# Seven products of combined operands in the second feed-forward projection of inner blocks, weight highs of those products on ScalarE

## Chip, cores, metric

One core of one Trainium2 chip. The metric is the device time of one execution in microseconds (us), as the median of several runs. All tensors are fp32. Engine names in profile rows: PE (TensorE matmul), PEld (TensorE weight load), DVE (VectorE), ACT (ScalarE), POOL (GpSimd), SPq (the queue from which SyncE issues DMAs). ps is PSUM.

## What is computed

A trunk of two layers (a Conformer convolution module, then an mLSTM) over 1024 prompt and 32 decode tokens. After its mixer each layer has the same squared-ReLU feed-forward network, with D_MODEL = 1024 and D_FF = 4096:

```
x = _layer_norm(DN_ALPHA * x + mix, p['ln_mix_g'][i], p['ln_mix_b'][i])
hid = jnp.square(jax.nn.relu(x @ p['ffn_w1'][i]))
x = _layer_norm(DN_ALPHA * x + hid @ p['ffn_w2'][i], p['ln_ffn_g'][i], p['ln_ffn_b'][i])
```

The change concerns only how `hid @ ffn_w2` is worked out.

## The kernel before

**Layout.** Activations stand transposed: the partition is the feature, the columns are the 1056 tokens, cut into three chunks of CW = 352 columns. X holds the residual stream in fp32.

**Precision.** An fp32 operand is used as two fp32r parts: a high part (a rounding copy) and a low part (the operand less its high part). A product of a 128x128 weight tile with 352 columns is three matmuls (`product`, L403 to L405): weight high by data high, weight high by data low, weight low by data high. AH, AL are the parts of the normalised input, HH, HL those of the hidden activations, WH, WL those of the weights.

**Weight panels.** SyncE loads a 512 KB panel into one of two raw buffers RAW (`load_panel`), GpSimd writes its high part into WH and then its low part into WL, each of 1024 columns (`split_panel`, L388 and L390), in one of four slots. Semaphores tie them: w_raw (panel landed), w_free (TensorE has released slots, counted by `free_panels`), w_split (low part written, which TensorE waits for).

**The feed-forward stage.** D_FF is cut into FB = 8 blocks of 512 hidden features. In each, the *hidden part* makes 12 outputs (3 chunks by 4 tiles) of 8 tile products, 12 x 24 = 288 matmuls; the *second part* makes 24 outputs (3 chunks by 8 tiles of 128 model features) of 4 tile products, 24 x 12 = 288 matmuls. Four panels serve the first and four the second. ScalarE takes the relu out of PSUM into SGF (L716) and squares it into HH (L718); VectorE squares SGF in fp32 into SQF (L733) and subtracts HH to get HL (L736). VectorE adds each output of the second part into X (L753). The eighth block (`last`) runs chunk by chunk with the layer normalisation woven in, and the first block (`first`) runs its hidden part chunk by chunk behind the normalisation before; blocks 1 to 6 are a loop.

**Order.** Every engine runs its own list in program order, written out by hand; there is no scheduler. On ScalarE a block is `ffn_act` (12 times relu, square), on GpSimd `ffn_splits` (8 panels, in the order of use), on VectorE `ffn_dve` (12 times square, low part; then 24 additions), on TensorE `ffn_pe`.

Of the kernel before, what the change touches and what calls it, by code (L numbers as in the profile page):

```python
# [53 lines left out]
def program(nc, a, o):  # L54
    with ExitStack() as ctx:
# [195 lines left out]
        WKR = at("WKR", [P, NJ, 4, 4], F32, O_S + 4096)  # L251
        QKP = at("QKP", [P, NJ, 4, 4], F32, O_S + 4096 + 1024)
# [14 lines left out]
        w_hi = sem("w_hi")  # L267
        w_split = sem("w_split")
# [63 lines left out]
        wd_hi, wd_lo, wd_mm, wd_acc = sem("wd_hi"), sem("wd_lo"), sem("wd_mm"), sem("wd_acc")  # L332
# [30 lines left out]

        class Ff:
# [3 lines left out]
            def __init__(self, n):  # L368
                self.nmm, self.nh, self.nacc = n * FB * 36, n * FB * 12, n * FB * 24
# [7 lines left out]
        def load_panel(sp, n, cnt, k, src, width):  # L377

            wait(sp, w_split, n - 1)
            sp.dma_start(RAW[:, k % 2].rearrange("p (k f) -> p k f", f=width), src).then_inc(w_raw[k % 2], 16)  # L380

        def split_panel(pool, n, cnt, k):
# [6 lines left out]
            wait(pool, w_hi, n + 1)  # L389
            pool.tensor_tensor(WL[:, k % 4], RAW[:, k % 2], WH[:, k % 4].bitcast(F32), ALU.subtract).then_inc(w_split, 1)  # L390
# [223 lines left out]
        NP_F = [24, 24 + 64 + 48]  # L614

        def pn(n0, k, b):
            return n0 + k + 8 * b, (n0 + k) // 2 + 1 + 4 * b

        def ffn_loads(sp, l, b):
            w1, w2 = a["ffn_w1"][l], a["ffn_w2"][l]  # L620
            for k in range(8):
                n, cnt = pn(NP_F[l], k, b)
# [4 lines left out]
                load_panel(sp, n, cnt, k, src.rearrange("(k p) f -> p k f", p=P), width)  # L627

        def ffn_splits(pool, l, b):
            for k in range(8):  # L630
                split_panel(pool, *pn(NP_F[l], k, b), k)

# [8 lines left out]

        def ffn_pe(pe, l, b, first, last, before=None):

            F = ff[l]
            L = (ln_m0, ln_m1)[l]
            for i, (c, u, h) in enumerate(hidden_order(first)):
                k = 2 * u + h
                if c == 0:
                    pe.wait_ge(w_split, pn(NP_F[l], k, b)[0] + 1)
                release = None  # L650
                if first:
# [22 lines left out]
            def hidden_ready(c):  # L674
                n = F.nh + 4 * c + 4 if first else F.nh + 12 * b + 6 + 2 * c + 2
                pe.wait_ge(F.relu, n)
                pe.wait_ge(F.hl, n)

            def unit(c, u, i, bank, between=None):

                k = 4 + u
                pe.wait_ge(w_split, pn(NP_F[l], k, b)[0] + 1)
                for h in range(2):
                    release = None
                    if h == 0 and (i == 0 or (c == 0 and not last) or (c == 2 and u and last)):
                        release = (F.mm, F.nmm + 36 * b + 12 + 2 * i, 2 if i == 0 else 1)
                    product(pe, bank(h), k % 4, 256, h, HH, HL, 4, ch[c], release).then_inc(F.mm, 1)
                    if h == 0 and between:
                        between(c, u)
            if last:  # L690
                def by_chunk(c, u, between):
                    i = 4 * c + u
                    if u == 0:
                        hidden_ready(c)
                    if i >= 2:
                        pe.wait_ge(F.acc, F.nacc + 24 * b + 2 * (i - 1))
                    unit(c, u, i, lambda h: bank_of(c, u, h), between)
                ln_pe(pe, (ln_f0, ln_f1)[l], by_chunk, 4, F.acc, F.nacc + 24 * b)
                free_panels(pe, F.mm, F.nmm + 36 * b + 36, 1)
            else:  # L700
                for u in range(4):
                    for c in range(3):
                        if u == 0:
                            hidden_ready(c)
                        else:
                            pe.wait_ge(F.acc, F.nacc + 24 * b + 6 * (u - 1) + 2 * c + 2)
                        unit(c, u, 3 * u + c, lambda h: 2 * c + h)

        def ffn_act(act, l, b, first=False):
            F = ff[l]  # L710
            L = (ln_m0, ln_m1)[l]
            for i, (c, u, h) in enumerate(hidden_order(first)):
                act.wait_ge(F.mm, F.nmm + 36 * b + i + 1)
                wait(act, F.sq, F.nh + 12 * b + i - 1)
                wait(act, F.hh, F.nh + 12 * b + i - 1)
                act.activation(SGF[:, i % 2], ps[:, hidden_bank(first, c, u, h), 0:CW], ACT.Relu).then_inc(F.relu, 1)  # L716
                act.wait_ge(F.relu, F.nh + 12 * b + i + 1)
                act.activation(HH[:, 2 * u + h, ch[c]], SGF[:, i % 2], ACT.Square).then_inc(F.hh, 1)  # L718
# [5 lines left out]
                if first and i >= 5 and i % 2:  # L724
                    ln_prescale(act, L, i // 2 - 2) if i < 11 else None

        def ffn_dve(dve, l, b, first=False, last=False):
            F = ff[l]
            L = (ln_m0, ln_m1)[l]
            for i, (c, u, h) in enumerate(hidden_order(first)):  # L730
                dve.wait_ge(F.relu, F.nh + 12 * b + i + 1)
                wait(dve, F.hl, F.nh + 12 * b + i - 1)
                dve.tensor_tensor(SQF[:, i % 2], SGF[:, i % 2], SGF[:, i % 2], ALU.mult).then_inc(F.sq, 1)  # L733
                dve.wait_ge(F.hh, F.nh + 12 * b + i + 1)
                dve.wait_ge(F.sq, F.nh + 12 * b + i + 1)
                dve.tensor_tensor(HL[:, 2 * u + h, ch[c]], SQF[:, i % 2], HH[:, 2 * u + h, ch[c]].bitcast(F32),  # L736
                                  ALU.subtract).then_inc(F.hl, 1)
# [1988 lines left out]
```

## Time and profile before

| | us |
|---|---|
| median of 3 runs | 3169.58 (3167.16 to 3170.78) |
| the profiled execution | 3167.34 |
| its span, first to last instruction | 3165.6 |
| TensorE busy in the span | 3055.3 (97%) |
| VectorE, ScalarE, GpSimd busy | 1586.9, 790.2, 830.0 |
| mean granted clock of TensorE | 0.99 |

The profile is one execution. A row of its list of groups gives line, engine, operation, output and inputs, shape and count, then total busy time and the mean of one in ns, then the idle time of the engine before them and what ended it. The matmuls' own durations overlap one another, so the pace of TensorE is read from their start times. A row of the timeline gives start, duration, engine, line and operation, and in square brackets how long the engine had been idle and what released it.

### The profile page before, as it was taken

How to read it: one execution, taken by the hardware profiler on the slowest of the kernel's cores; microseconds unless marked ns; L12 is line 12 of the kernel's file. 1: busy time of each engine (PE TensorE's matmuls, PEld its weight loads, DVE VectorE, ACT ScalarE, POOL GpSimd, SP SyncE). 2: the span in 40 equal slices, each digit the busy share in tenths (PEclk: the TensorE clock that was granted, in tenths of full speed). 3: DMA queues.
4: the chain of work that ended last, by engine and by line, in shares of the span. 5: the costliest groups of instructions: out<-in, count | busy, mean ns of one | idle time of the engine just before them, and what ended most of it. 6: DMA issues, size and time to landing. Idle time of an engine off the chain costs nothing.

```text
span 3165.6 us, 50120 instructions
## 1 busy us (share of the span) xinstructions
PE 3055.3 (97%) x20024; PEld 2841.0 (90%) x20024; DVE 1586.9 (50%) x2318; ACT 790.2 (25%) x1475; POOL 830.0 (26%) x523
## 2 busy tenths in 40 slices
PE   7998899999999999999989999998999999999997
PEld 7885789999999998999967878777999999999996
DVE  4877454333333354443358687878227333333335
ACT  4000442011111124111144444534106111111113
POOL 2232113333323232333201110113414232333330
PEclk9999999999999999999989999999999999999999
DMA  7555311111111113323255564747311111111111
GB/s 217 148 133 138 94 33 54 47 46 46 46 40 50 43 41 119 119 101 114 85 181 205 203 237 179 251 162 278 102 35 54 41 53 40 53 46 46 46 34 55
DMA packets 277968, 317.92 MB, mean 100 GB/s; under 512 B 25877, under 2 KB 217621, under 8 KB 276610
## 3 DMA queue, kind: packets, MB, share of 16 engines
q1 hardware_dynamic: 257577, 250.01, 25.6%
q10 hardware_dynamic: 12960, 40.04, 3.3%
q0 software_dynamic: 7296, 25.96, 2.4%
q8 instruction: 98, 1.61, 0.2%
q14 instruction: 37, 0.30, 0.0%
HBM read 224.63 MB, written 92.19 MB: 100 GB/s over the span
## 4 chain that ended last, share of the span: by engine, by line
PE 79%; DVE 10%; ACT 6%; issue 4%; DMA 1%; SPq 0%; POOL 0%; another core or an unknown queue 0%; DVEq 0%; ACTq 0%; POOLq 0%
PE ps L403 23%; PE ps L404 22%; PE ps L405 22%; PE ps L2068 2%; PE ps L1128 2%; PE ps L1171 1%; DVE CB L2489 1%; ACT X L486 1%; DVE CT L1565 1%; PE ps L1137 1%; PE ps L1138 1%; DVE RST L1729 1%; PE ps L1139 1%; PE ps L424 1%; DVE HT L1747 1%
## 5 line engine op out<-in xcount | busy, mean ns | idle before, releaser
L403 PE MATMUL ps<-AH,WH 128*128 128x352 f32 x3072 | 1000.4, 326 | 6.2 <-ACT SO L849 4.1
L404 PE MATMUL ps<-AL,WH 128*128 128x352 f32 x3072 | 986.2, 321 | 0.0
L405 PE MATMUL ps<-AH,WL 128*128 128x352 f32 x3072 | 985.7, 321 | 0.0
L388 POOL TENSOR_SCALAR WH<-RAW 128x1024 fp32r<-128x1024 f32 x200 | 236.0, 1180 | 1663.5 <-PEq L410 1467.7
L403 PEld LDWEIGHTS ps<-AH,WH 128*128 128x128 f32 x3072 | 577.6, 188 | 31.5 <-issue 22.6
L404 PEld LDWEIGHTS ps<-AL,WH 128*128 128x128 f32 x3072 | 578.7, 188 | 1.1 <-issue 0.2
L405 PEld LDWEIGHTS ps<-AH,WL 128*128 128x128 f32 x3072 | 577.5, 188 | 0.0
L390 POOL TENSOR_TENSOR WL<-RAW,WH 128x1024 fp32r<-128x1024 f32 x200 | 517.3, 2587 | 16.7
L403 PE MATMUL ps<-HH,WH 128*128 128x352 f32 x1536 | 498.4, 324 | 0.0
L404 PE MATMUL ps<-HL,WH 128*128 128x352 f32 x1536 | 492.2, 320 | 0.0
L405 PE MATMUL ps<-HH,WL 128*128 128x352 f32 x1536 | 491.9, 320 | 0.0
L753 DVE TENSOR_TENSOR X<-X,ps 128x352 f32<-128x352 f32 x384 | 198.0, 520 | 465.7 <-PE ps L405 465.7
L716 ACT ACTIVATE SGF<-ps 128x352 f32<-128x352 f32 x192 | 89.1, 464 | 1121.9 <-PE ps L405 1121.8
L733 DVE TENSOR_TENSOR SQF<-SGF 128x352 f32<-128x352 f32 x192 | 137.5, 716 | 388.9 <-ACT SGF L716 388.6
L403 PEld LDWEIGHTS ps<-HH,WH 128*128 128x128 f32 x1536 | 288.1, 188 | 5.4 <-issue 4.6
L404 PEld LDWEIGHTS ps<-HL,WH 128*128 128x128 f32 x1536 | 288.6, 188 | 0.8
L405 PEld LDWEIGHTS ps<-HH,WL 128*128 128x128 f32 x1536 | 287.9, 187 | 0.0
L736 DVE TENSOR_TENSOR HL<-SQF,HH 128x352 fp32r<-128x352 f32 x192 | 197.1, 1027 | 20.0
L2489 DVE SCALAR_TENSOR_TENSOR CB<-U,PR,CB 128x32 f32<-128x32 f32 (+3 forms) x180 | 157.3, 934 | 0.7
L1171 PE MATMUL ps<-QT,XCH 128*128 128x256 f32 (+1 forms) x640 | 137.0, 358 | 0.0
L1171 PEld LDWEIGHTS ps<-QT,XCH 128*128 128x128 f32 x640 | 112.9, 190 | 13.8
L905 DVE SCALAR_TENSOR_TENSOR XC<-XM,PRM,XC 128x1024 f32<-128x1024 f32 x96 | 106.6, 1167 | 0.0
(317 smaller groups left out, 3392.3 us busy)
## 6 DMA issues: line engine op xcount, KB each, us to landing
RAW<-in_ffn_w SPq DMA_DIRECT2D x128, 512.0 KB, 3.6
CT<-in_state_mlstm_C SPq DMA_DIRECT2D x32, 1024.0 KB, 5.5
out_C_s<-CT SPq DMA_DIRECT2D x32, 1024.0 KB, 5.4
RAW<-in_ml_w_in SPq DMA_DIRECT2D x32, 512.0 KB, 3.9
RAW<-in_conv_w_pw SPq DMA_DIRECT2D x24, 512.0 KB, 7.9
STK<-u_scratch SPq DMA_DIRECT2D x64, 184.0 KB, 3.8
xc_scratch<-XC ACTq DMA_DIRECT2D x16, 528.0 KB, 2.7
so_scratch<-SO ACTq DMA_DIRECT2D x16, 528.0 KB, 3.7
```

Of the source, the lines that this page charges most:

```text
L388: pool.tensor_scalar(WH[:, k % 4], RAW[:, k % 2], 1.0, 0.0, ALU.mult, ALU.add).then_inc(w_hi, 1)
L390: pool.tensor_tensor(WL[:, k % 4], RAW[:, k % 2], WH[:, k % 4].bitcast(F32), ALU.subtract).then_inc(w_split, 1)
L403: pe.matmul(ps[:, bank, 0:CW], wh[:, k, cols], hi[:, k, cs], start=(k == 0), stop=False)
L404: pe.matmul(ps[:, bank, 0:CW], wh[:, k, cols], lo[:, k, cs], start=False, stop=False)
L405: mm = pe.matmul(ps[:, bank, 0:CW], wl[:, k, cols], hi[:, k, cs], start=False, stop=(k == nk - 1))
L716: act.activation(SGF[:, i % 2], ps[:, hidden_bank(first, c, u, h), 0:CW], ACT.Relu).then_inc(F.relu, 1)
L733: dve.tensor_tensor(SQF[:, i % 2], SGF[:, i % 2], SGF[:, i % 2], ALU.mult).then_inc(F.sq, 1)
L736: dve.tensor_tensor(HL[:, 2 * u + h, ch[c]], SQF[:, i % 2], HH[:, 2 * u + h, ch[c]].bitcast(F32), ALU.subtract).then_inc(F.hl, 1)
L753: dve.tensor_tensor(x, x, ps[:, bank, 0:CW], ALU.add).then_inc(F.acc, 1)
L905: ins = dve.scalar_tensor_tensor(o_, x_, PRM[:, j, t:t + 1], o_, ALU.mult, ALU.add)
L1171: mm = pe.matmul(ps[:, 3 + q % 2, o_:256], xch(h)[:, dt, i * P:(i + 1) * P], QT[:, dt, tc * 256 + o_:tc * 256 + 256], start=(dt == 0), sto ...
L2489: ins = dve.scalar_tensor_tensor(y, x(t), w, y, ALU.mult, ALU.add)
```

## The change

In blocks 0 to 6 of both layers (14 blocks), the second part treats chunks 0 and 1 together. For each pair of output tiles (four pairs a block, numbered g) the 2x2 block product [two output tiles] by [two chunks] is made with seven products M1 to M7 of combined operands in place of eight, each over two 128-deep tiles (6 matmuls where the eight had 6 each). Chunk 2 keeps two ordinary products of 12 matmuls (P0, P1). A pair is 7 x 6 + 2 x 12 = 66 matmuls, before 72.

**Weights.** For each pair GpSimd no longer makes both parts. ScalarE makes the high part of the plain panel (`corner_highs`, called at the end of `ffn_act`), GpSimd its low part, then four small operations of 128x256 that form the combined corners in RAW itself; ScalarE makes the high part of these and GpSimd their low part, in a second slot. A block has 12 panels of four slots where it had 8.

**Activations.** VectorE writes the squares to HR (the place of HL), forms combined tiles (`combine`), and writes low parts with larger operations; ScalarE rounds the combined tiles (`combined_highs`).

**Sums.** M1 is added to X and then M6, M7 and M4 go on in the same PSUM bank, each being added to another tile of X after the next product has joined. A pair has 9 additions where it had 6.

The buffers WKR and QKP of the block weights moved to other addresses, and the counts of semaphores changed everywhere accordingly.

```diff
+        def ffn_splits(pool, l, b, last=False):
+            for k in range(8 if last else 4):
+                split_panel(pool, panel_no(l, b, k), panel_in(l, b, k) // 16, k, split_no(l, b, k))
+            for g in range(0 if last else 4):
...
+                a11, a12, a21, a22 = (corner(raw, j, i) for i in range(2) for j in range(2))
+                pool.wait_ge(a_hi, na + 1)
+                pool.tensor_tensor(WL[:, 2 * g % 4], raw, WH[:, 2 * g % 4].bitcast(F32), ALU.subtract).then_inc(w_split, 1)
+                pool.wait_ge(w_split, n + 1)
+                pool.tensor_tensor(a22, a21, a22, ALU.add).then_inc(w_hi, 1)
+                pool.wait_ge(w_hi, q + 1)
+                pool.tensor_tensor(a21, a11, a21, ALU.subtract).then_inc(w_hi, 1)
...
+                pool.tensor_tensor(a12, a12, a11, ALU.subtract).then_inc(w_hi, 1)
+                pool.wait_ge(w_hi, q + 4)
+                pool.wait_ge(a_hi, na + 2)
+                pool.tensor_tensor(WL[:, (2 * g + 1) % 4], raw, WH[:, (2 * g + 1) % 4].bitcast(F32), ALU.subtract).then_inc(w_split, 1)
+
+        def corner_highs(act, l, b):
+
+            for g in range(4):
+                k, n, q = 4 + g, panel_no(l, b, 4 + 2 * g), split_no(l, b, 4 + 4 * g)
+                act.wait_ge(w_raw[k % 2], panel_in(l, b, k))
+                act.wait_ge(w_free, n - 3)
+                act.copy(WH[:, 2 * g % 4], RAW[:, k % 2]).then_inc(a_hi, 1)
+                act.wait_ge(w_hi, q + 4)
+                act.wait_ge(w_free, n - 2)
+                act.copy(WH[:, (2 * g + 1) % 4], RAW[:, k % 2]).then_inc(a_hi, 1)
...
+            def m1(g):
+                slot = weights(g, 0)
+                if g == 0:
+                    pe.wait_ge(F.relu, relu0 + (11 if first else 10))
+                    operand("corner")
...
+                added(g - 2, "M4")
+                seven(xbank(g), slot, 0, 0, *tile(0, 0), True, (F.mm, mm0 + 12, 2) if g == 0 else None)
+
+            def m4(g):
+                added(g, "M7")
+                operand("t")
+                seven(xbank(g), 2 * g % 4, 1, 1, *combined(1), False)
+
+            def m2(g):
+                added(g - 1, "M2")
+                seven(YB, 2 * g % 4, 1, 0, *tile(1, 0), True, (F.mm, mm0 + 12 + turn(g - 1, "M4") + 1, 2) if g else None)
+
+            def m5(g):
+                slot = weights(g, 1)
+                operand("t1")
+                added(g - 1, "M3")
+                seven(ZB, slot, 1, 1, *tile(0, 1), True)
...
+            for g in range(4):
+                m1(g)
+                if g:
+                    m4(g - 1)
+                m2(g)
+                m5(g)
+                plain(g, 0)
+                m6(g)
+                m3(g)
+                plain(g, 1)
+                m7(g)
+            m4(3)
...
+            if not last:
+                corner_highs(act, l, b)
...
+                dve.tensor_tensor(t3, b22, b12, ALU.subtract).then_inc(F.sq, 1)
+                dve.tensor_tensor(b12, b12, b11, ALU.subtract).then_inc(F.sq, 1)
...
+                dve.tensor_tensor(t2, b22, b12, ALU.subtract).then_inc(F.sq, 1)
...
+                dve.tensor_tensor(t4, b21, t2, ALU.subtract).then_inc(F.sq, 1)
...
+                low(HL[:, both, ch[0]], HR[:, both, ch[0]], HH[:, both, ch[0]])
...
+                low(HL[:, 2 * u, ch[1]], HR[:, 2 * u, ch[1]], HH[:, 2 * u, ch[1]])
...
+                low(TL[:, :, u], TR[:, :, u], TH[:, :, u])
+                low(HL[:, 2 * u + 1, ch[1]], HR[:, 2 * u + 1, ch[1]], HH[:, 2 * u + 1, ch[1]])
```

**What stands where.** ScalarE, the end of a block in the loop of layer 0, before: the last two relus (L716) and squares (L718), behind which the loop turns to the next block.

```order
234 L717 REGISTER_ALU
235 L718 ACTIVATE HH<-SGF 128x352 [waits ffn_relu]
236 L713 REGISTER_ALU
237 L716 ACTIVATE SGF<-ps 128x352 [waits ffn_hh,ffn_sq,ffn_mm]
238 L717 REGISTER_ALU
239 L718 ACTIVATE HH<-SGF 128x352 [waits ffn_relu]
240 L2350 REGISTER_ALU
241 L2350 COMPARE_AND_BRANCH
```

ScalarE at the same place, now. L906 and L909 are the relu and the square; L684 to L689 are `corner_highs`, of which the first of four pairs is shown, the next following at once.

```order
266 L901 REGISTER_ALU [waits ffn_mm]
267 L902 REGISTER_ALU [waits ffn_sq]
268 L906 ACTIVATE SGF<-ps 128x352 [waits ffn_hh]
269 L908 REGISTER_ALU
270 L909 ACTIVATE HH<-SGF 128x352 [waits ffn_relu]
271 L684 ISA
272 L685 REGISTER_ALU [waits w_raw0]
273 L686 CAST WH<-RAW 128x1024 [waits w_free]
274 L687 REGISTER_ALU
275 L688 REGISTER_ALU [waits w_hi]
276 L689 CAST WH<-RAW 128x1024 [waits w_free]
```

All eight roundings of the block's second-part weights stand behind the relu and square of its last hidden output.

GpSimd, the second half of the loop's body, before: the last three of four panels of the second part, each a high part (L388) that needs only a raw panel and a free slot, and a low part.

```order
80 L388 TENSOR_SCALAR WH<-RAW 128x1024 [waits w_free,w_raw1]
81 L51 REGISTER_ALU
82 L390 TENSOR_TENSOR WL<-RAW,WH 128x1024 [waits w_hi]
83 L51 ISA [waits w_free]
84 L388 TENSOR_SCALAR WH<-RAW 128x1024 [waits w_raw0]
85 L51 REGISTER_ALU
86 L390 TENSOR_TENSOR WL<-RAW,WH 128x1024 [waits w_hi]
87 L388 TENSOR_SCALAR WH<-RAW 128x1024 [waits w_free,w_raw1]
88 L51 REGISTER_ALU
89 L390 TENSOR_TENSOR WL<-RAW,WH 128x1024 [waits w_hi]
90 L1955 REGISTER_ALU
91 L1955 COMPARE_AND_BRANCH
```

GpSimd, the first pair's panel, now (L667 low part of the plain panel, L669 to L675 the combined corners, L678 their low part).

```order
109 L667 TENSOR_TENSOR WL<-RAW,WH 128x1024 [waits a_hi]
110 L668 REGISTER_ALU
111 L669 TENSOR_TENSOR RAW<-RAW 128x2x128 [waits w_split]
112 L670 REGISTER_ALU
113 L671 TENSOR_TENSOR RAW<-RAW 128x2x128 [waits w_hi]
114 L672 REGISTER_ALU
115 L673 TENSOR_TENSOR RAW<-RAW 128x2x128 [waits w_hi]
116 L674 REGISTER_ALU
117 L675 TENSOR_TENSOR RAW<-RAW 128x2x128 [waits w_hi]
118 L676 REGISTER_ALU
119 L677 REGISTER_ALU [waits w_hi]
120 L678 TENSOR_TENSOR WL<-RAW,WH 128x1024 [waits a_hi]
```

Each low part now waits for a_hi, the count of ScalarE's roundings, and the corners stand between the two low parts.

## Rows read from the trace of the kernel before

**Rows 1.** The page: span, busy time by engine, granted clock in 40 slices.

```profile
span 3165.6 us, 50120 instructions
...
PE 3055.3 (97%) x20024; PEld 2841.0 (90%) x20024; DVE 1586.9 (50%) x2318; ACT 790.2 (25%) x1475; POOL 830.0 (26%) x523
...
PEclk9999999999999999999989999999999999999999
```

**Rows 2.** Busy time in the halves of one block: window, length, then each engine.

```profile
541.66:587.42 45.76, 45.76 (x290) 45.76 (x290) 20.84 (x27) 11.57 (x24) 10.94 (x6) 1.00 0.12 35
587.42:633.22 45.80, 45.80 (x290) 45.80 (x290) 12.78 (x25) 0.00 (x1) 17.59 (x11) 1.00 0.20 58
```

**Rows 3.** Timeline, TensorE, from the hidden part into the second part.

```profile
583.12 0.32 PE L405 MATMUL ps<-AH,WL 128*128 128x352 f32 x1
583.28 0.32 PE L403 MATMUL ps<-HH,WH 128*128 128x352 f32 x1
```

**Rows 4.** Timeline, ScalarE: the block's last relu and square, the next block's first relu.

```profile
583.48 0.47 ACT L716 ACTIVATE SGF<-ps 128x352 f32<-128x352 f32 x1 [2.82 <-PE ps L405]
583.98 0.50 ACT L718 ACTIVATE HH<-SGF 128x352 fp32r<-128x352 f32 x1
633.22 0.47 ACT L716 ACTIVATE SGF<-ps 128x352 f32<-128x352 f32 x1 [48.74 <-PE ps L405]
```

**Rows 5.** Timeline, GpSimd: one panel of the second part.

```profile
595.29 1.05 POOL L388 TENSOR_SCALAR WH<-RAW 128x1024 fp32r<-128x1024 f32 x1 [4.01 <-PEq L410]
596.42 2.40 POOL L390 TENSOR_TENSOR WL<-RAW,WH 128x1024 fp32r<-128x1024 f32 x1
```

**Rows 6.** Groups by line and shape, whole run: durations for new operations.

```profile
L2269 ACT CAST AH<-X 128x1024 fp32r<-128x1024 f32 x8 | 8.4, 1048 | 0.3
...
L390 POOL TENSOR_TENSOR WL<-RAW,WH 128x1024 fp32r<-128x1024 f32 x200 | 517.3, 2587 | 16.7
...
L1945 POOL TENSOR_TENSOR SEL<-SEL,ident 128x32 f32<-128x32 f32 x2 | 0.5, 252 | 0.2
...
L494 DVE TENSOR_TENSOR AL<-X,AH 128x1408 fp32r<-128x1408 f32 x18 | 30.2, 1680 | 28.7 <-ACT AH L490 28.7
L1593 DVE TENSOR_TENSOR PL<-PT,PH 128x256 fp32r<-128x256 f32 x64 | 28.4, 444 | 1.9 <-ACT PH L1376 1.9
```

**Rows 7.** Timeline, TensorE: the first matmuls behind three longer waits.

```profile
1220.58 0.63 PE L403 MATMUL ps<-AH,WH 128*128 128x352 f32 x1 [4.08 <-ACT SO L849]
...
2184.79 0.49 PE L403 MATMUL ps<-AL,WH 128*128 128x352 f32 x1 [3.46 <-POOL WL L390]
...
2214.92 0.40 PE L403 MATMUL ps<-AL,WH 128*128 128x352 f32 x1 [4.00 <-POOL WL L390]
```

**Rows 8.** Timeline, GpSimd: the low parts that ended two of those waits.

```profile
2180.85 3.69 POOL L390 TENSOR_TENSOR WL<-RAW,WH 128x1024 fp32r<-128x1024 f32 x1
...
2212.43 2.34 POOL L390 TENSOR_TENSOR WL<-RAW,WH 128x1024 fp32r<-128x1024 f32 x1
```

**Rows 9.** Timeline, VectorE, one block: a low part alone, one beside GpSimd, an addition.

```profile
546.46 0.53 DVE L736 TENSOR_TENSOR HL<-SQF,HH 128x352 fp32r<-128x352 f32 x1
...
585.34 2.54 DVE L736 TENSOR_TENSOR HL<-SQF,HH 128x352 fp32r<-128x352 f32 x1
...
589.21 0.52 DVE L753 TENSOR_TENSOR X<-X,ps 128x352 f32<-128x352 f32 x1 [0.47 <-PE ps L405]
```

**Rows 10.** Windows behind those three waits; the third value from the right is the clock.

```profile
2188.00:2190.00 2.00, 2.00 (x12) 1.95 (x12) 1.55 (x6) 1.00 (x2) 0.49 (x1) 0.91 1.05 448
...
2214.00:2216.00 2.00, 1.08 (x6) 1.11 (x7) 0.00 (x0) 0.00 (x0) 1.92 (x3) 0.92 1.06 397
...
2218.00:2220.00 2.00, 2.00 (x11) 2.00 (x10) 0.00 (x0) 0.00 (x0) 0.24 (x1) 0.73 1.07 401
...
1224.00:1226.00 2.00, 2.00 (x9) 2.00 (x8) 0.00 (x0) 2.00 (x2) 0.00 (x0) 0.55 0.00 0
```

**Rows 11.** The page's DMA issues: panels of the feed-forward weights.

```profile
RAW<-in_ffn_w SPq DMA_DIRECT2D x128, 512.0 KB, 3.6
```

More of the change, by code:

```diff
@@ L626, in ffn_loads @@
                     src, width = w2[bass.ds(b * 512, 512), (k - 4) * 256:(k - 3) * 256], 256
[L627 to L631, printed above, removed]
+                if last or k < 6:
+                    done = n + k - 1 if k or (isinstance(b, int) and b == 0) else n - 2
+                else:
+                    done = n + 2 * k - 6
@@ L672, in ffn_pe, with hidden_ready @@
                     ln_var_sum(pe, L, 2)
[L674 to L689, printed above, removed]
             if last:
+                def hidden_ready(c):
+                    n = 6 + 2 * c + 2
+                    pe.wait_ge(F.relu, relu0 + n)
+                    pe.wait_ge(F.hl, hl0 + n)
                 def by_chunk(c, u, between):
                     i = 4 * c + u
+                    k = 4 + u
                     if u == 0:
@@ L695, in by_chunk @@
                     if i >= 2:
[L696 to L707, printed above, removed]
@@ L709, in ffn_act @@
-        def ffn_act(act, l, b, first=False):
+                        pe.wait_ge(F.acc, acc0 + 2 * (i - 1))
+                    pe.wait_ge(w_split, panel_no(l, b, k) + 1)
+                    for h in range(2):
+                        release = None
+                        if h == 0 and (i == 0 or (c == 2 and u)):
+                            release = (F.mm, mm0 + 12 + 2 * i, 2 if i == 0 else 1)
+                        product(pe, bank_of(c, u, h), k % 4, 256, h, HH, HL, 4, ch[c], release).then_inc(F.mm, 1)
+                        if h == 0:
+                            between(c, u)
@@ new lines, in ffn_pe, with seven @@
+                ln_pe(pe, (ln_f0, ln_f1)[l], by_chunk, 4, F.acc, acc0)
+                free_panels(pe, F.mm, mm0 + 36, 1)
+                return
+            def seven(bank, slot, j, i, hi, lo, start, release=None):
+                for k in range(2):
+                    if k == 1 and release:
+                        free_panels(pe, *release)
+                    wh, wl = corner(WH[:, slot], j, i)[:, k], corner(WL[:, slot], j, i)[:, k]
+                    pe.matmul(ps[:, bank, 0:CW], wh, hi(k), start=(start and k == 0), stop=False, skip_group_check=True)
+                    pe.matmul(ps[:, bank, 0:CW], wh, lo(k), start=False, stop=False, skip_group_check=True)
+                    mm = pe.matmul(ps[:, bank, 0:CW], wl, hi(k), start=False, stop=(k == 1), skip_group_check=True)
+                mm.then_inc(F.mm, 1)
@@ new lines, in ffn_dve @@
+            for i, (c, u, h) in enumerate(hidden_order(first)):
+                dve.wait_ge(F.relu, relu0 + i + 1)
+                if last:
+                    wait(dve, F.hl, hl0 + i - 1)
+                    dve.tensor_tensor(SQF[:, i % 2], SGF[:, i % 2], SGF[:, i % 2], ALU.mult).then_inc(F.sq, 1)
+                    dve.wait_ge(F.hh, hh0 + i + 1)
+                    dve.wait_ge(F.sq, sq0 + i + 1)
+                    dve.tensor_tensor(HL[:, 2 * u + h, ch[c]], SQF[:, i % 2], HH[:, 2 * u + h, ch[c]].bitcast(F32),
+                                      ALU.subtract).then_inc(F.hl, 1)
+                else:
+                    dve.tensor_tensor(raw(2 * u + h, c), SGF[:, i % 2], SGF[:, i % 2], ALU.mult).then_inc(F.sq, 1)
+                    if (c, h) == (1, 1):
+                        if l and first and u == 0:
+                            dve.wait_ge(d_out, 16 * (8 + HEADS))
+                        combine(u, i)
+                    if (c, h) == (2, 1):
+                        both = slice(2 * u, 2 * u + 2)
+                        dve.wait_ge(F.sq, sq0 + raw_order(first, i) + 1)
+                        dve.wait_ge(F.hh, hh0 + squared(first, i))
+                        low(HL[:, both, ch[2]], HR[:, both, ch[2]], HH[:, both, ch[2]])
@@ L2349, in _ @@
             ffn_act(act, 0, 0, True)
-            with act.Fori(1, FB) as b:
+            with act.Fori(1, FB - 1) as b:
                 ffn_act(act, 0, b)
+            ffn_act(act, 0, FB - 1, last=True)
             ln_act(act, ln_f0, R_FFNG, R_FFNB, 4)
```

272 lines of the change are left out of this document (204 added, 68 removed).

## Prediction, made before the changed kernel had run

> **What bounds the kernel now.** I read the page first: TensorE is busy 97% of the span and its clock is full nearly throughout; no other engine is busy more than half of it [rows 1]. Next, the windows of one block in the loop of layer 0: it takes 633.22 − 541.66 = 91.56 us, and TensorE is busy for all of both halves [rows 2, 4]. A block has 576 matmuls, so one costs 91.56/576 = 0.159 us, which is also the distance of two start times [rows 3]. So inside these blocks only two things count: how many matmuls there are, and whether TensorE ever waits. In the timeline it does not: the second part's first matmul follows the hidden part's last without a gap [rows 3], because the low part of its panel had long been made. GpSimd makes each panel one or two ahead, as soon as TensorE frees a slot, in 1.05 + 0.08 + 2.40 = 3.53 us [rows 5].
>
> **What the change removes.** Each pair loses 6 matmuls, a block 24, the kernel 14 x 24 = 336: 14 x 3.82 = 53.4 us. That is all it can win.
>
> **What it adds on TensorE's path: the first pair of each block.** I count time from the moment at which the second part would start, 583.28 in the trace before. The roundings of the weights now stand on ScalarE behind the block's last relu and square. That relu cannot start before TensorE has ended the hidden part: it starts at 0.20, and the square ends at 583.98 + 0.50 − 583.28 = 1.20 [rows 4]. Raw panel and slots were ready long before, but ScalarE comes to them only now. Then, in series:
> - high part, 1024 columns on ScalarE, 1.05 [rows 6]: from 1.25 to 2.30.
> - low part on GpSimd, 2.40 [rows 5]: from 2.36 to 4.76.
> - GpSimd to TensorE 0.15: the first row of [rows 7] that waited on a quiet low part began 0.15 after it (2214.92 against 2212.43 + 2.34, [rows 8]). M1 starts at **4.91** instead of 0.
> - the four corner operations of 256 columns. No row shows them; between 0.252 for 32 columns and 2.40 for 1024 a straight line gives 0.252 + 224 x 2.148/992 = 0.74, and with the group's mean of 2.59 it gives 0.78 [rows 5, 6]. I take 0.78 and 0.08 between two: 4.84 to 8.20. Bounds: 0.65 (a quarter of 2.59) and 1.05 (what 1024 columns with one input cost [rows 5]).
> - ScalarE high part, 8.27 to 9.32; GpSimd low part, 9.38 to 11.78. M5, which needs this second slot, starts at **11.93**.
> Without waits M5 would start 12 matmuls after M1, at 1.91. The pair is **10.02 us** late; 4.91 before M1 and 5.11 between M2 and M5.
>
> The Trainium skill, GPSIMD Engine Reference, section "Elementwise — side-by-side cycle accounting", gives 2.6 cycles at 1.2 GHz for each element of a two-input operation, from which I estimate 0.55 + 0.18 = 0.73 us a piece; the sum would be 14 x 4 x 0.05 = 3 us less. Its section "Engine selection" says that two-input elementwise work belongs to VectorE, about twice as fast. This speaks against the change: VectorE takes 0.44 for such a piece [rows 6], which would save 1.4 us of each of these waits, 19 us in all, had the change put them there.
>
> **The other pairs.** Slots of pair g+1 are freed behind the first matmuls of M2 of pair g, as GpSimd's release now comes 0.57 into a product (595.29 [rows 5], against 583.28 + 72 x 0.159 = 594.72). From there the same series runs: 0.57 + 0.05 + 1.05 + 0.07 + 2.40 + 4 x 0.86 + 0.07 + 1.05 + 0.07 + 2.40 + 0.15 = 11.32. M5 of pair g+1 comes 66 + 6 matmuls after that M2 starts, at 11.45. So it is just in time, by 0.13 us: no stall, but no cover either. Every 0.1 us more for a corner piece costs 0.3 to 0.4 in each of pairs 2 and 3. Pair 1 has slots free since M1 of pair 0 and is ready at 21.4 where M5 is due at 22.4.
>
> **The sums.** M4 of a pair must wait until M7's addition is done: 0.20 from the product's nominal end to the addition and 0.52 for it (589.21 is 0.20 behind the second product's end, 583.28 + 36 x 0.159 = 589.01 [rows 9]), 0.05 back: 0.77. In pairs 0 to 2 M1 of the next pair, 0.95, hides that; behind the last pair nothing does: **0.77 us** a block. The other additions have two products or more as cover. Their 36 x 0.52 = 19 us on VectorE lie beside 42 us of matmuls.
>
> **Activations.** VectorE has four more operations in each half of the hidden part, and ScalarE one rounding of 1056 columns. The last `combine` starts after output 10 of 12, at −7.6 (two products before the end). Relu, square, four operations of 0.53, then low parts of 704, 352, 1056 and 352 columns at 0.91, 0.53, 1.30, 0.53 (from 0.53 and 1.68 by a line [rows 6, 9]) end at about −0.6, and the rest, square 10, square 11 and the low part of chunk 2, at 2.3. All is before 4.91, and GpSimd starts at 2.36, so that VectorE is not held up beside it as in the row where a low part took 2.54 [rows 9]. This costs nothing, hidden by the wait for the weights; without that wait P0, the first to need chunk 2's low part, would start at 18 x 0.159 = 2.9, so it would cost nothing either. SyncE's loads come 3.6 us after issue [rows 11] and are asked for when a raw buffer's second low part is made, some 10 us ahead of use: nothing.
>
> **The clock.** Behind each of three waits of 3.46, 4.00 and 4.08 us the clock was 0.5 for a while, that is 1.2 of 2.4 GHz, and a matmul then cost 0.29. A window's mean tells how much of it was at half: 0.91 over 2 us is 0.36 us. So the low stretches that lay on busy time ran from 2184.79 to 2188.36, from 2215.7 to 2219.1 and from 1220.58 to 1225.8 [rows 7, 10]; half of each is lost: 1.8, 1.7, 2.6 us. The two new waits, 4.9 and 5.1 with only 12 matmuls between them, are longer than all of these. What M1 and M2 lose is hidden, since M5 waits for a fixed moment. Behind M5 I take **2.3 us**, to the upper end since two waits stand together; bounds 0 and 2.6. None of the three was spared, so I count all 14 blocks.
>
> The Trainium skill has a rule on it (TensorE: Matmul & The Clock Gate, section "HAM oscillation — how this bites in real kernels"): a loop that waits long in each turn pays for a fall of the clock in each turn. By it the sum would hold the clock's term 14 times too, and the rival without it has no place; the trace agrees in three of three waits.
>
> **The sum.** A block: −3.82 + 10.02 + 0.77 + 2.3 = +9.27 us; fourteen: +129.8. First blocks run their hidden part in another order, but their weights stand behind the last relu too, so I count them alike. The profiled execution was 3167.34, so 3297.1 for it; the median lies 2.2 above that execution: **3299 us**, 4% slower.
>
> **Rivals.**
> - *The clock stays up* (the waits are shorter than I think, or the fall passes while TensorE waits). For: in the second row of three the first matmuls were still at the full clock. Against: three of three in [rows 7, 10]. 14 x 2.3 = 32 less: 3267. Chance 0.13.
> - *The second slot's series is the bound in every pair.* With corner pieces at 1.05, each series is 1.08 longer: +1.1 in pair 0, and 11.32 + 1.08 − 11.45 = 0.95 in pairs 2 and 3: 3.0 a block, 42 in all: 3341. For: operations with short rows and two inputs that nobody timed, and a margin of 0.13. Against: the line through two rows. Half of it is as likely as the whole. Chance 0.13.
> - *The other side: weights in time.* If ScalarE made the first pair's roundings before its last relu, M1 and M5 would not wait, nor the clock fall: −3.82 + 0.77 a block, 3127. For: the panel lies in RAW and slots are free some 20 us ahead. Against: the order on ScalarE's list, which no wait can change. It turns to a gain where the waits in a block are under 3.8 us together; M1's alone is over that. Chance 0.03; no change, 0.01.
>
> **How the numbers follow.** Forecast 0.70. The range goes from a little under the rival without the clock's fall, 3258, to the dear corner pieces, 3340. A measurement of this kernel can tell about 0.2% from no change. Faster 0.03, same 0.01, slower 0.96.
>
> **What would show it.** Right: in each of 14 blocks TensorE idle twice, about 5 and (at a low clock less, 3.5) us, both put down to GpSimd's low part; 12 matmuls between; the clock below 1 behind; ScalarE's first rounding directly behind its last square; a loop's block of about 101 us. Wrong: a second-part start without idle time, idle time at M5 of later pairs, or the wait put down to VectorE's tiles or to a DMA.

## Result and the profile after

| | us |
|---|---|
| before, median of 4 runs | 3169.03 (3167.16 to 3170.78) |
| after, median of 4 runs | 3304.19 (3300.08 to 3309.79) |
| ratio | 1.0423, 95% interval 1.0411 to 1.0436 |
| span of the profiled execution, before and after | 3165.6, 3302.5 |

The change costs 135 us. It was to cost 130 (3299, range 3258 to 3340).

The page of the changed kernel, answering [rows 1]: 336 matmuls fewer (20024 less 19688), GpSimd and ScalarE busier, and TensorE busy for a smaller share of a longer span.

```profile
span 3302.5 us, 50982 instructions
...
PE 3068.2 (93%) x19688; PEld 2837.5 (86%) x19688; DVE 1643.8 (50%) x2570; ACT 930.9 (28%) x1615; POOL 1060.1 (32%) x747
```

TensorE's waits, longest groups first. Where [rows 3] had no gap there are now 14 of each kind: M1's (L667 is the plain low part), M5's (L678 the low part of the combined corners) and M4's (L1000 an addition). A line gives the time in total, how often, and the longest.

```profile
PE ps L786 <- POOL WL L667: 69.5, 14, 6.4
PE ps L786 <- POOL WL L678: 41.9, 14, 3.2
...
PE ps L786 <- DVE X L1000: 9.6, 14, 0.7
```

One block of the loop in layer 0, in the timelines. The last matmul of the hidden part:

```profile
797.78 0.32 PE L418 MATMUL ps<-AH,WL 128*128 128x352 f32 x1
```

The prediction's zero, 583.28, was the moment at which the second part would start, one distance of 0.16 behind the start of that matmul. Here it is 797.94, and every lateness below counts from there. Now ScalarE: the last relu and square, and behind them both roundings of pair 0 and the first of pair 1, in answer to [rows 4].

```profile
798.30 0.46 ACT L906 ACTIVATE SGF<-ps 128x352 f32<-128x352 f32 x1 [2.49 <-PE ps L418]
798.79 0.50 ACT L909 ACTIVATE HH<-SGF 128x352 fp32r<-128x352 f32 x1
799.20 1.03 ACT L686 CAST WH<-RAW 128x1024 fp32r<-128x1024 f32 x1
805.98 1.05 ACT L689 CAST WH<-RAW 128x1024 fp32r<-128x1024 f32 x1 [5.75 <-POOL RAW L675]
806.93 1.04 ACT L686 CAST WH<-RAW 128x1024 fp32r<-128x1024 f32 x1
```

GpSimd at the same place, answering [rows 5]. It had been idle for 40 us, and the last transfer of the panels that lay ready in RAW had ended at 764.

```profile
800.30 2.34 POOL L667 TENSOR_TENSOR WL<-RAW,WH 128x1024 fp32r<-128x1024 f32 x1 [40.48 <-ACT WH L686]
802.72 0.72 POOL L669 TENSOR_TENSOR RAW<-RAW 128x256 f32<-128x256 f32 x1
803.52 0.73 POOL L671 TENSOR_TENSOR RAW<-RAW 128x256 f32<-128x256 f32 x1
804.33 0.73 POOL L673 TENSOR_TENSOR RAW<-RAW 128x256 f32<-128x256 f32 x1
805.14 0.73 POOL L675 TENSOR_TENSOR RAW<-RAW 128x256 f32<-128x256 f32 x1
807.10 2.34 POOL L678 TENSOR_TENSOR WL<-RAW,WH 128x1024 fp32r<-128x1024 f32 x1 [1.23 <-ACT WH L689]
```

TensorE: the first matmul of M1, of M5, and of the last M4.

```profile
802.86 0.66 PE L786 MATMUL ps<-HH,WH 128*128 128x352 f32 x1 [4.75 <-POOL WL L667]
...
809.57 0.66 PE L786 MATMUL ps<-HH,WH 128*128 128x352 f32 x1 [3.20 <-POOL WL L678]
...
851.47 0.43 PE L786 MATMUL ps<-TH,WH 128*128 128x352 f32 x1 [0.70 <-DVE X L1000]
```

Read the three together: the hand-over goes TensorE, ScalarE's relu and square, ScalarE's rounding, GpSimd, TensorE, then GpSimd's corners, ScalarE, GpSimd, TensorE, and nothing in it overlaps the hidden part. M1 starts 4.92 late, and M5 11.63 behind the hidden part's end instead of 1.91. (The idle times in brackets are shorter, 4.75 and 3.20, since they count from the recorded end of a matmul and not from where the next would have started.) Over five blocks of the loop, first matmul of M1 at 601.50 to the same at 1106.47, a block takes 100.99 us where it took 91.56.

In the two first blocks M1 starts 6.3 and 6.5 late and M5 13.1 and 13.3. A scaling of X stands there on ScalarE's list ahead of the last two relus, and so ahead of the first rounding:

```profile
492.99 2.54 ACT L513 ACTIVATE X<-X 128x2816 f32<-128x2816 f32 x1
```

```profile
500.69 0.66 PE L786 MATMUL ps<-HH,WH 128*128 128x352 f32 x1 [6.10 <-POOL WL L667]
```

From the hidden part's end to the end of M4 these two blocks take 56.4 and 56.1 us where they took 45.8.

The clock around M5 (window, length, five engines, clock, DMA share, GB/s), answering [rows 10]:

```profile
809.00:811.00 2.00, 1.43 (x5) 1.44 (x6) 0.00 (x0) 0.00 (x0) 2.00 (x2) 0.55 0.11 36
811.00:813.00 2.00, 2.00 (x10) 2.00 (x9) 0.52 (x1) 0.00 (x0) 1.84 (x3) 0.60 0.67 226
813.00:815.00 2.00, 2.00 (x14) 2.00 (x13) 0.52 (x1) 0.00 (x0) 1.84 (x3) 1.00 0.00 0
```

M5 begins at 1.2 GHz and the clock is back at 2.4 some 3 us later.

### The profile page after: what moved, and what is told of

Same layout as the page of the kernel before. It is cut to its first block, busy times and chain, and to the rows that moved or that the text cites. A ratio compares the mean times of both kernels' runs of the same rounds, so it can differ in the third digit from the quotient of the medians.

```text
span 3302.5 us, 50982 instructions
## 1 busy us (share of the span) xinstructions
PE 3068.2 (93%) x19688; PEld 2837.5 (86%) x19688; DVE 1643.8 (50%) x2570; ACT 930.9 (28%) x1615; POOL 1060.1 (32%) x747
## 4 chain that ended last, share of the span: by engine, by line
PE 55%; issue 20%; DVE 11%; ACT 7%; POOL 5%; DMA 1%; PEld 0%; POOLq 0%; SPq 0%; another core or an unknown queue 0%; DVEq 0%; PEldq 0%; ACTq 0%
PE ps L416 11%; PE ps L417 11%; PE ps L418 11%; PE ps L786 4%; PE ps L787 4%; PE ps L788 4%; PE ps L2326 2%; PE ps L1421 1%; PE ps L1378 1%; ACT X L499 1%; DVE CB L2749 1%; POOL WL L403 1%; POOL WL L667 1%; POOL WL L678 1%; DVE CT L1815 1%
## 5 line engine op out<-in xcount | busy, mean ns | idle before, releaser
L1000 DVE TENSOR_TENSOR X<-X,ps 128x352 f32<-128x352 f32 x504 | 262.7, 521 | 483.8 <-PE ps L788 316.8
L401 POOL TENSOR_SCALAR WH<-RAW 128x1024 fp32r<-128x1024 f32 x144 | 174.0, 1208 | 835.3 <-PEq L423 637.5
L403 POOL TENSOR_TENSOR WL<-RAW,WH 128x1024 fp32r<-128x1024 f32 x144 | 377.6, 2623 | 12.0
L667 POOL TENSOR_TENSOR WL<-RAW,WH 128x1024 fp32r<-128x1024 f32 x56 | 133.4, 2381 | 650.6 <-ACT WH L686 650.6
L786 PE MATMUL ps<-HH,WH 128*128 128x352 f32 x448 | 162.7, 363 | 111.4 <-POOL WL L667 69.5
L966 DVE TENSOR_TENSOR HR<-SGF 128x352 f32<-128x352 f32 x168 | 89.7, 538 | 347.5 <-ACT SGF L906 347.3
L906 ACT ACTIVATE SGF<-ps 128x352 f32<-128x352 f32 x192 | 88.3, 462 | 610.3 <-PE ps L418 610.3
L416 PE MATMUL ps<-HH,WH 128*128 128x352 f32 x640 | 216.7, 339 | 0.0
L417 PE MATMUL ps<-HL,WH 128*128 128x352 f32 x640 | 212.0, 331 | 0.0
L418 PE MATMUL ps<-HH,WL 128*128 128x352 f32 x640 | 211.7, 331 | 0.0
L786 PEld LDWEIGHTS ps<-HH,WH 128*128 128x128 f32 x448 | 94.7, 211 | 120.7 <-issue 100.9
L788 PE MATMUL ps<-HH,WL 128*128 128x352 f32 x448 | 157.9, 352 | 0.0
L787 PE MATMUL ps<-HL,WH 128*128 128x352 f32 x448 | 157.8, 352 | 0.0
L678 POOL TENSOR_TENSOR WL<-RAW,WH 128x1024 fp32r<-128x1024 f32 x56 | 133.8, 2390 | 68.9 <-ACT WH L689 68.9
L689 ACT CAST WH<-RAW 128x1024 fp32r<-128x1024 f32 x56 | 58.7, 1049 | 344.6 <-POOL RAW L675 344.6
```

Of the source, the lines that this page charges most:

```text
L416: pe.matmul(ps[:, bank, 0:CW], wh[:, k, cols], hi[:, k, cs], start=(k == 0), stop=False)
L417: pe.matmul(ps[:, bank, 0:CW], wh[:, k, cols], lo[:, k, cs], start=False, stop=False)
L418: mm = pe.matmul(ps[:, bank, 0:CW], wl[:, k, cols], hi[:, k, cs], start=False, stop=(k == nk - 1))
L667: pool.tensor_tensor(WL[:, 2 * g % 4], raw, WH[:, 2 * g % 4].bitcast(F32), ALU.subtract).then_inc(w_split, 1)
L678: pool.tensor_tensor(WL[:, (2 * g + 1) % 4], raw, WH[:, (2 * g + 1) % 4].bitcast(F32), ALU.subtract).then_inc(w_split, 1)
L786: pe.matmul(ps[:, bank, 0:CW], wh, hi(k), start=(start and k == 0), stop=False, skip_group_check=True)
```

## Experiments

Each is the changed kernel with the edit shown, or one of these variants with one edit more, where the text says so. Times are medians, each compared with runs of the kernel before on the same chip. The variants ran on two chips, on which the kernel before took 3172.2 and 3169.2 us, so a difference in us between two variants can be off by some 3; the ratios allow for it.

### Who rounds: GpSimd instead of ScalarE

```diff
+                pool.wait_ge(w_raw[k % 2], panel_in(l, b, k))
+                pool.wait_ge(w_free, n - 3)
...
+                pool.tensor_scalar(WH[:, 2 * g % 4], raw, 1.0, 0.0, ALU.mult, ALU.add).then_inc(a_hi, 1)
                 pool.wait_ge(a_hi, na + 1)
...
                 pool.wait_ge(w_hi, q + 4)
+                pool.wait_ge(w_free, n - 2)
...
+                pool.tensor_scalar(WH[:, (2 * g + 1) % 4], raw, 1.0, 0.0, ALU.mult, ALU.add).then_inc(a_hi, 1)
                 pool.wait_ge(a_hi, na + 2)
...
-            if not last:
-                corner_highs(act, l, b)
```

> The changed kernel, but GpSimd makes the high parts of the second part's panels too, as it did before the change; ScalarE has none. Products, sums and activations are those of the change. Theory (the hand-over through ScalarE, whose list reaches it only behind the last relu, holds up M1 and M5 of pair 0): in the loop's blocks pair 0 is ready about 12 us ahead and both waits and the clock's fall go; a block costs -3.82 + 0.87 (M4's wait as the trace of after has it) = -2.95 us against before. In the two first blocks slots come free two products before the end only, so that M5 still waits some 1.6 us. 3169 - 41 + 3 = 3131. Rival (GpSimd's series itself, or its contention with VectorE's combining, is the bound): GpSimd has 1.05 us more twice a pair, so every later pair waits too: 3304 or more.

**Measured: 3190.34 us**, ratio 1.006 (1.0044 to 1.0077). Both waits are gone from the loop's blocks and 114 us with them, so the rival falls. But it stopped 59 us above the 3131 expected. The trace shows one new wait in each loop block, at P0. TensorE, then VectorE and GpSimd around it:

```profile
685.40 0.43 PE L416 MATMUL ps<-HH,WH 128*128 128x352 f32 x1 [1.88 <-DVE HL L939]
```

```profile
682.49 2.85 DVE L939 TENSOR_TENSOR HL<-HR,HH 128x704 fp32r<-128x704 f32 x1
```

```profile
682.08 2.52 POOL L672 TENSOR_TENSOR WL<-RAW,WH 128x1024 fp32r<-128x1024 f32 x1
684.68 1.26 POOL L674 TENSOR_TENSOR RAW<-RAW 128x256 f32<-128x256 f32 x1
```

The block's last low part on VectorE, for which P0 waits, takes 2.85 us instead of 0.89, lying beside GpSimd's low part of pair 1, which now starts as soon as M1 frees slots. It is what [rows 9] showed at 2.54 where nobody waited for it. The expectation had left it out. A loop block takes 91.0 us, or 92.6 where the clock falls behind the wait (8 of 12), against 88.6 expected: some 41 of the 59 us. The rest lies in the two first blocks, where P0 waits 4.8 us for the same low part and M1 2.35.

### Is that the sharing?

The variant above with one wait more: GpSimd begins the panel of pair 1 only behind VectorE's last low part.

```diff
                 pool.wait_ge(w_raw[k % 2], panel_in(l, b, k))
+                if g == 1:
+                    pool.wait_ge(ff[l].hl, ff[l].nhl + 10 * b + 10)
```

> gpsimd_highs with one wait more: GpSimd begins the panel of pair 1 only when VectorE has made its last low part of the block (chunk 2, second half). Theory (in gpsimd_highs that low part, 0.89 us alone, took 2.85 beside GpSimd's low part of pair 1, so that P0 waited 1.88 us, and the clock's fall behind it cost about 1.6 more): both go; pair 1 is begun some 1.5 us later, which its margin of about 1.3 us nearly takes. 12 loop blocks x 3.4 = 41 less, up to 0.3 of them back: 3190 - 41 + (0 to 4) = 3149 to 3153. Rival (VectorE is late by its own work, not by the sharing): 3190 or more.

**Measured: 3159.69 us**, ratio 0.9974 (0.9965 to 0.9983), 31 us less than without the hold (27 by the ratios). The low part is back at its own length, and the wait at P0 is gone:

```profile
679.23 0.89 DVE L941 TENSOR_TENSOR HL<-HR,HH 128x704 fp32r<-128x704 f32 x1
```

So it was the sharing, not VectorE's own work: a GpSimd instruction put later made the kernel faster. The gain is less than the 41 expected for two reasons that the trace shows. Another 0.75 to 0.80 us of idle time appears in each loop block some 13 us behind the hidden part's end (at 601.10, 691.12, 781.13), at M5 of pair 1: its panel is now begun later, and the panel's second low part ends 0.13 ahead of it. (The profile puts the wait down to an addition that ends 0.02 later, for which M5 does not wait.) And the clock had fallen behind that wait of 1.88 in 8 of 12 loop blocks only.

```profile
598.60 2.37 POOL L689 TENSOR_TENSOR WL<-RAW,WH 128x1024 fp32r<-128x1024 f32 x1
```

```profile
601.10 0.43 PE L797 MATMUL ps<-HH,WH 128*128 128x352 f32 x1 [0.75 <-DVE X L1009]
```

A loop block takes 90.0, 2.05 less on the mean, or 25 us in all. Some 8 more come from the two first blocks, which the expectation had not counted: P0's wait of 4.8 us there is 0.4 and 0.7 now.

### Where on ScalarE's list

ScalarE keeps the roundings; only the place of pair 0's two moves.

```diff
+                if not last and i == (10 if first else 6):
+                    corner_high(act, l, b, 0, 0)
+                if not last and i == (11 if first else 8):
+                    corner_high(act, l, b, 0, 1)
...
             if not last:
-                corner_highs(act, l, b)
+                for g in range(1, 4):
+                    corner_high(act, l, b, g, 0)
+                    corner_high(act, l, b, g, 1)
```

> The changed kernel with the two ScalarE roundings of pair 0 moved up on ScalarE's list: in the loop's blocks behind the squares of hidden outputs 7 and 9, in first blocks behind those of outputs 11 and 12 (there the slots come free no sooner). Nothing else. Theory (the place on the list alone is the fault): loop blocks as with GpSimd's highs, -2.95 us; first blocks keep a wait of about 6 us at M5 and 1.5 us of low clock, +15 us in all; 3169 - 41 + 15 = 3143. Rival (moving them delays the relus and the combined activations as much, since ScalarE waits for GpSimd's corners at the second): stays over 3200.

**Measured: 3158.69 us**, ratio 0.9959 (0.9945 to 0.9973): 145 us less than the changed kernel, by two instructions a block that stand elsewhere, and faster than the kernel before. In the loop's blocks TensorE's only wait is M4's. TensorE's waits in this kernel:

```profile
PE ps L787 <- POOL WL L667: 10.2, 2, 5.2
PE ps L787 <- DVE X L1007: 9.6, 14, 0.7
...
PE ps L787 <- POOL WL L678: 7.2, 2, 3.6
```

Of the 15 us above the 3143 expected some 12 lie in the two first blocks, where M1 and M5 still wait 5.2 and 3.6: I had thought M1 free there. The last pairs of outputs come close together, and ScalarE has a scaling of X (2.55 us) between them. The rest is 0.3 us in each loop block, 88.93 where 88.6 was expected.

### The two waits apart

Only the first rounding moved (`i == 6`, in first blocks 10), the second left behind the last square.

> Only the first rounding of pair 0 is moved up (behind the square of hidden output 7; in first blocks of output 11); the second stays behind the last square. It tells the two waits apart. Theory: M1 waits no more; M5 is ready at 1.25 + 1.05 + 0.05 + 2.40 + 0.15 = 4.9 where it is due at 1.91, a wait of 2.9 us. If a wait of 2.9 us costs no clock, a loop block is -3.82 + 0.87 + 2.9 = -0.05 and the whole about 3178 (first blocks +4.5 each); if it does, 1.5 us more in each of 12 blocks, 3196. Rival (the two waits are one delay, and what M1 gains M5 loses): 3290 to 3304.

**Measured: 3203.77 us**, ratio 1.0109 (1.0089 to 1.0129). M1 does not wait in the loop's blocks, M5 waits 2.8 to 3.1 us; so they are two delays, each with its own hand-over, and the rival falls. M5 of pair 0 in three blocks in a row:

```profile
693.77 0.66 PE L787 MATMUL ps<-HH,WH 128*128 128x352 f32 x1 [2.87 <-POOL WL L678]
...
787.30 0.42 PE L787 MATMUL ps<-HH,WH 128*128 128x352 f32 x1 [2.86 <-POOL WL L678]
...
879.50 0.42 PE L787 MATMUL ps<-HH,WH 128*128 128x352 f32 x1 [2.86 <-POOL WL L678]
```

The clock fell behind the first of these waits and not behind the others. So the block from 693.77 takes 93.53 us and that from 787.30 takes 92.20: the fall alone costs 1.3 here. It came in 3 of 12 loop blocks only, so neither of my two numbers is met, and the mean of four blocks (693.77 to 1063.89) is 92.53. Against the 91.5 expected even a block without the fall is 0.7 more: M4's wait was counted, but not the slower first matmul behind each wait (0.27 us to the next start instead of 0.16, 0.45 where the clock is low), the 0.1 by which an idle time in brackets is shorter than the delay, and some 0.4 in hundredths. Over 12 loop blocks that is 12 of the 26 us above 3178. Most of the rest lies in the two first blocks, which take 10.3 more than before between the hidden part's end and M4's, where I had counted 4.5.

### The clock

28 matmuls of no use, whose results nobody reads, ahead of M1 and of M5 of pair 0:

```diff
+            def fill(n):
+                pe.wait_ge(F.relu, relu0 + (11 if first else 11))
+                for _ in range(n):
+                    pe.matmul(ps[:, 4, 0:CW], AH[:, 0, 0:P], AH[:, 0, ch[0]], start=True, stop=True, skip_group_check=True)
...
             def m1(g):
+                if g == 0:
+                    fill(28)
...
             def m5(g):
+                if g == 0:
+                    fill(28)
```

> The changed kernel with 28 matmuls of no use ahead of M1 and 28 ahead of M5 of pair 0 in every block, 4.45 us each at full clock, on operands that are ready (AH) and into a PSUM bank that nobody reads. They fill the waits of 4.76 us and keep TensorE at work, but wait for nothing new. Theory (the clock falls because TensorE stands idle, and costs 1.3 to 2.3 us a block behind M5): M5 starts at the same moment, the clock stays at 1.0, 3304 - 14 x (1.3 to 2.3) = 3272 to 3286. Rival (the low clock costs nothing, the excess lies in waits): 3304. If the filler itself is late: above 3304.

**Measured: 3279.17 us**, ratio 1.0338 (1.0316 to 1.036). 784 more matmuls made the kernel 25 us faster, 1.8 a block. In the same stretch of a block, hidden part's end to behind M5, the clock stays whole:

```profile
690.00:700.00 10.00, 9.97 (x63) 9.68 (x61) 5.91 (x10) 4.34 (x7) 2.30 (x1) 1.00 0.00 0
700.00:704.00 4.00, 3.68 (x23) 3.69 (x24) 1.04 (x2) 0.54 (x1) 3.04 (x5) 1.00 0.00 0
704.00:708.00 4.00, 3.86 (x24) 3.58 (x23) 0.00 (x0) 1.46 (x2) 3.41 (x2) 1.00 0.00 0
```

So the clock is a cost of its own, and idle TensorE its cause. In the trace of the changed kernel 8 to 19 matmuls behind the 14 M5 waits start 0.29 apart, 178 in all, or 12.7 a block, each 0.134 too long: 1.7 us, which fits the 1.8. (All that the start distances behind M5 have over 0.159, the slow first one included, is 2.1 a block; filled, the first distance is still 0.26, and M5 starts 0.16 later, at 11.79.) Those that M1 and M2 lose are hidden, as the wait for the second slot only grows without them.

### The series behind M5

```diff
-                pool.tensor_tensor(a22, a21, a22, ALU.add).then_inc(w_hi, 1)
+                pool.tensor_tensor(a22[:, :, 0:16], a21[:, :, 0:16], a22[:, :, 0:16], ALU.add).then_inc(w_hi, 1)
```

and so for the other three. Seven eighths of that work is left out, and the combined corners are no longer the algorithm's.

> The changed kernel, but each of GpSimd's four corner operations treats 2x16 columns where it treats 2x128, so that the combined corners are not those of the algorithm. It leaves out seven eighths of that work and nothing of the order. Theory (M5's wait is a series in which each of the four operations counts): each falls from 0.735 to about 0.25, M5 of pair 0 comes 1.9 us earlier, 14 x 1.9 = 27 less, 3304 - 27 = 3277, and as the wait shortens a little of the clock's loss may go too (down to 3262). Rival (M5 waits for an operand or a bank): 3304.

**Measured: 3275.92 us** (two runs), ratio 1.0338 (1.0319 to 1.0357), 28 less. Each corner operation takes 0.25, and M5's wait is 0.94 instead of about 3:

```profile
798.00 0.25 POOL L669 TENSOR_TENSOR RAW<-RAW 128x32 f32<-128x32 f32 x1
```

```profile
798.15 0.66 PE L786 MATMUL ps<-HH,WH 128*128 128x352 f32 x1 [4.76 <-POOL WL L667]
802.98 0.66 PE L786 MATMUL ps<-HH,WH 128*128 128x352 f32 x1 [0.94 <-POOL WL L678]
```

All that the four lose, 4 x 0.48, comes off M5's start (4.83 behind M1's instead of 6.71) and the total, while M1's wait is untouched: it is a series, as computed.

### M4's wait, and the first blocks

`scalar_early` with M7 ahead of P1 in TURN, in TensorE's list and in VectorE's:

```diff
-        TURN = ("M1", "M4", "M2", "M5", "P0", "M6", "M3", "P1", "M7")
+        TURN = ("M1", "M4", "M2", "M5", "P0", "M6", "M3", "M7", "P1")
```

> scalar_early with M7 made and added before the second product of chunk 2 (P1) in every pair, where it stood behind it. Theory (M4 of the last pair waits 0.70 us for M7's addition and costs 0.87 to 1.0 a block with the slower start behind it; P1, 1.9 us, now covers it; M7 itself needs M6's addition, 0.77, under M3's 0.95): 14 x 0.9 = 12 less than scalar_early, 3146. Rival (M7 now waits for M6's addition in each pair by a hop more than M3 covers): no change, or worse by 4 x 0.1 a block.

**Measured: 3144.44 us**, ratio 0.9921 (0.9907 to 0.9934). 14 us less than `scalar_early` (12 by the ratios); no gap over 0.15 us is left on TensorE in the second parts of the loop's blocks, in either layer.

In the two first blocks, the first rounding of pair 0 moved up as well:

```diff
-                if not last and i == (10 if first else 6):
+                if not last and i == (8 if first else 6):
```

> early_m7_first with the first rounding of pair 0 in the two first blocks moved up too, from behind the square of hidden output 11 to behind that of output 9, ahead of one of ScalarE's long scalings of X (2.55 us); the second stays behind the last. Theory (in first blocks ScalarE's list still holds M1 up, 5.24 us in the trace of scalar_early, then M5 by 3.6): M1's wait goes or is under 1.5 us, M5 stays about where the second rounding puts it, some 3 to 4 us earlier: 2 x (3 to 5) = 6 to 10 less, 3136 to 3140. Rival (the block's first slots are not free so early): 3146.

**Measured: 3139.73 us**, ratio 0.9906 (0.9891 to 0.9921), about 5 us less, a little under the least expected. In the first block of layer 0 M1's wait falls from 5.22 to 2.33, more than the 1.5 expected, and M5's rises from 3.60 to 4.39:

```profile
497.48 0.40 PE L787 MATMUL ps<-HH,WH 128*128 128x352 f32 x1 [2.33 <-issue]
504.04 0.66 PE L787 MATMUL ps<-HH,WH 128*128 128x352 f32 x1 [4.39 <-POOL WL L678]
```

The weights' low part, made by 496.16, no longer holds M1 up. M1 also waits for the relu of output 11, and that one ends at 497.38, behind the scaling of X:

```profile
494.50 2.53 ACT L513 ACTIVATE X<-X 128x2816 f32<-128x2816 f32 x1
496.94 0.44 ACT L907 ACTIVATE SGF<-ps 128x352 f32<-128x352 f32 x1
```

M5 starts 3.8 and 4.1 earlier behind the hidden part's end in the two blocks, as expected. In the profiled executions that makes 8 us; the medians differ by 5, and five runs of `early_m7_first` alone lie 6 apart.

This is the fastest of all, 29 us under the kernel before. Of 53.4 us that 336 matmuls are worth, 24 are still lost, part of it in these two blocks.

## Where the prediction was right and where not

| step, us a block | predicted | measured |
|---|---|---|
| 24 matmuls fewer | −3.82 | 336 fewer in all; 0.159 each in the hidden part, 0.161 in the second |
| M1 behind the hidden part's end | 4.91 | 4.92 in loop blocks, 6.3 and 6.5 in first |
| M5 behind the hidden part's end | 11.93 | 11.63 in loop blocks, 13.1 and 13.3 in first |
| lateness of the pair by both | 10.02 | 9.72 |
| last M4 | 0.77 | 0.70 idle, 0.87 between the starts, 0.98 with the slower start behind |
| a corner operation | 0.78 (0.65 to 1.05) | 0.735 |
| second slot ahead of M5, pairs 2 and 3 | 0.13 | 0.9 and 0.8 (block at 797.94) |
| clock behind M5 | 2.3 (0 to 2.6) | 1.7 by count, 1.8 by filling |
| one loop block against before | +9.27 | +9.43 |
| one first block against before | +9.27 | +10.6 and +10.3, from the hidden part's end on |

**Right, by experiment.** That ScalarE's place on the list holds up pair 0: moving two roundings took back 145 us. That each of the two waits is a series with its own hand-over (`second_late`, `small_corners`). That the idle time brings the clock down and that this costs beside the waits (`filled_waits`). That M4's wait is uncovered only at the last pair, and goes when P1 stands behind M7. **Right, by the trace.** Pairs 1 to 3 do not wait in the changed kernel: in the second part of none of the 14 blocks is there an idle time over 0.15 us but those of M1 and M5 of pair 0 and of the last M4.

**Mis-sized.** M5 came 0.30 earlier than computed: a corner operation takes 0.735 (the line through the two rows alone had given 0.74, the mean of a group that held disturbed ones 0.78), and GpSimd's low part 2.34. M1 at 4.92 for 4.91 is two errors that cancel: the last relu starts 0.36 behind the hidden part's end and not 0.20, and the rounding starts at 1.26, 0.09 ahead of the square's recorded end and not 0.05 behind it. The clock's term was 0.5 too high; the argument that two waits in a row put it to the upper end was wrong. What balances them are terms I had none for: 0.1 to 0.3 us for the first matmul behind the waits of M5 and M4, 0.1 on M4's wait, and some 0.4 a block in hundredths, since the second part's matmuls start 0.1608 apart on the mean and not 0.1590. They do not lie at the heads of the products, and their cause is open. First blocks cost some 1.1 us more each than loop blocks, where I had counted them alike: ScalarE's scaling of X delays the last relus. So the close total owes something to luck.

**Rivals.** The clock did fall. The second slot's series did not become the bound of later pairs. The rival on the other side, weights in time, priced at 3127, is what `scalar_early` built: it gave 3159, and 3140 with both other edits. Its mechanism was right; its price left out the first blocks, in which ScalarE's scalings of X stand between the outputs. By the trace they make some 27 of the 32 us that `scalar_early` lies above it.

**Activations cost nothing**, as predicted, but only since GpSimd was late. The sentence that they would cost nothing without the weights' wait either, by a margin of 0.6 us, holds where ScalarE rounds. It failed in `gpsimd_highs`, by 1.88 us at P0: GpSimd, started earlier, met VectorE's last low part.

## To carry to other kernels

Work handed to an idle engine takes its place in that engine's list; what counts is what stands ahead of it there, not how busy the engine is. ScalarE was busy for a quarter of the span and still cost 135 us, since its new work stood behind an instruction that TensorE itself had to release. Before judging a saving in matmuls, follow the first operand behind the change from engine to engine, and look where each link of that chain can begin at the earliest.

## What the runs showed of the hardware

**VectorE beside GpSimd.** A VectorE operation with two SBUF inputs, 0.89 us alone, took 2.85 beside a GpSimd operation of 2.52; the changed kernel's additions, one input in PSUM, took 0.52 throughout, also beside GpSimd. The VectorE operation started 0.41 behind GpSimd's and ended 0.74 behind its end, which is nearly its own length: this looks like waiting for the whole of the other, not like sharing, but no run tests it. The Trainium skill states this (GPSIMD Engine Reference, section "Specifications": the SBUF interfaces are shared, with contention for VectorE instructions that have two SBUF inputs), and the traces agree.

**A fall of the clock is not told by the wait before it alone.** Behind waits of 4.76 us it was low in every loop block; behind one of 1.88 in 8 of 12, behind those of 2.8 to 3.1 in 3 of 12. What follows a fall varies too: 8 to 19 matmuls at 1.2 GHz behind M5 in the changed kernel. An estimate for one place should therefore be a mean over many, and its bound for a single block wide.

**Useless matmuls can pay.** 56 of them a block in waits that were there anyway returned 1.8 us. The better repair is to remove the wait.
